# Forty projection tiles in blocks of seven half-depth products in place of eight

## The reference, cut to what matters

```python
h = rms_norm(x, norm_g[layer])
proj = h @ w_in[layer]              # 2048 x 1024 @ 1024 x 8704
u_ssm, z_ssm, q, k, v, z_attn, q_mem, z_mem, gate_logits = split(proj)
y = s5_ssm(u_ssm, ...); y = gelu(y); y = y * sigmoid(y @ w_glu + b_glu)
o_ssm = y * silu(z_ssm)
o_attn = dilated_window_attention(q, k, v) * silu(z_attn)
o_mem = softmax(q_mem @ k_mem.T) @ v_mem * silu(z_mem)
gates = sigmoid(gate_logits + b_gate)
merged = gates[0] * (o_ssm @ w_br_ssm) + gates[1] * (o_attn @ w_br_attn) + gates[2] * (o_mem @ w_br_mem)
x = x + merged @ w_out
return rms_norm(x, final_norm_g)
```

## Time and profile before

| | before |
|---|---|
| median of 3 runs | 2456.7 us (2455.96 to 2456.8) |
| span of the profiled execution | 2455.0 us |
| PE busy, granted clock | 99% of the span, 1.00 in all slices |
| DVE, ACT, POOL busy | 57%, 24%, 8% |
| ACT empties tiles 28 to 43 (64 units, SiLU) | first starts at 686.9, last at 1114.8 us |
| ACT empties tiles 44 to 67 (96 units, gates) | first starts at 1122.3, last at 1817.2 us |

### The profile page before, as it was taken

How to read it: one execution, slowest core, us unless ns; L and a number is a source line. 1 busy time by engine, 2 the same in 40 slices (tenths; PEclk the granted TensorE clock), 3 DMA queues, 4 the chain that set the end, 5 groups by cost and what they waited for, 6 DMA issues and landing times.

```text
span 2455.0 us, 31834 instructions
## 1 busy us (share of the span) xinstructions
PE 2438.3 (99%) x12622; PEld 1981.9 (81%) x12622; DVE 1397.7 (57%) x2636; ACT 588.0 (24%) x1275; POOL 190.4 (8%) x328
## 2 busy tenths in 40 slices
PE   9999999999999999999999999999999999999998
PEld 8888888888877777787777788888888888888887
DVE  7356776767734444413544443444345778787785
ACT  5222222222211111113333343333251111110201
POOL 0000000000011111110000000011100000000000
PEclk9999999999999999999999999999999999999999
DMA  8232433343454444442332343477654865857571
GB/s 327 99 93 76 106 114 117 107 120 95 115 151 137 149 160 142 151 156 73 105 134 95 121 147 122 161 228 243 205 206 164 285 182 168 248 177 242 159 233 59
DMA packets 171033, 378.67 MB, mean 154 GB/s; under 512 B 27008, under 2 KB 72164, under 8 KB 163717
## 3 DMA queue, kind: packets, MB, share of 16 engines
q1 hardware_dynamic: 134980, 235.03, 31.0%
q0 software_dynamic: 34864, 139.51, 16.9%
q10 hardware_dynamic: 1040, 2.10, 0.2%
HBM read 245.10 MB, written 131.43 MB: 153 GB/s over the span
## 4 chain that ended last, share of the span: by engine, by line
PE 97%; DVE 1%; ACT 1%; issue 0%; DMA 0%; DVEq 0%; SPq 0%; ACTq 0%
PE bank L137 29%; PE bank L139 29%; PE bank L138 28%; PE bank L2285 2%; PE bank L2328 1%; PE bank L2306 1%; PE bank L2194 1%; PE bank L2197 1%; PE bank L2264 1%; PE bank L2180 1%; PE bank L2242 1%; PE bank L2316 1%; ACT tsc L1188 1%; PE bank L2145 0%; PE bank L2247 0%
## 5 line engine op out<-in xcount | busy, mean ns | idle before, releaser
L137 PE MATMUL bank<-h_hi,w_hi 128*128 128x512 f32 (+1 forms) x2720 | 1083.7, 398 | 1.4 <-DVE h_lo L1434 1.4
L139 PE MATMUL bank<-h_hi,w_lo 128*128 128x512 f32 (+1 forms) x2720 | 1057.4, 389 | 0.0
L138 PE MATMUL bank<-h_lo,w_hi 128*128 128x512 f32 (+1 forms) x2720 | 1056.3, 388 | 0.0
L137 PEld LDWEIGHTS bank<-h_hi,w_hi 128*128 128x128 f32 x2720 | 510.8, 188 | 117.2 <-issue 13.6
L139 PEld LDWEIGHTS bank<-h_hi,w_lo 128*128 128x128 f32 x2720 | 510.7, 188 | 108.1
L138 PEld LDWEIGHTS bank<-h_lo,w_hi 128*128 128x128 f32 x2720 | 511.3, 188 | 103.0 <-issue 1.7
L129 DVE CAST w_hi<-w_raw 128x1024 fp32r<-128x1024 f32 (+1 forms) x121 | 83.3, 688 | 310.1 <-PE bank L139 294.3
L137 PE MATMUL bank<-h_hi 128*128 128x512 f32 (+1 forms) x464 | 172.5, 372 | 2.7 <-issue 1.5
L139 PE MATMUL bank<-h_hi,h_lo 128*128 128x512 f32 (+1 forms) x464 | 170.4, 367 | 0.0
L138 PE MATMUL bank<-h_lo,h_hi 128*128 128x512 f32 (+1 forms) x464 | 170.3, 367 | 0.0
L956 POOL DMA_DIRECT2D proj_d<-ev x160 | 88.9, 556 | 931.5 <-ACT ev L1148 560.1
(11 more groups left out here) (267 smaller groups left out, 2166.6 us busy)
## 6 DMA issues: line engine op xcount, KB each, us to landing
proj_d<-ev POOLq DMA_DIRECT2D x160, 256.0 KB, 2.9
w_raw<-w_in SPq DMA_DIRECT2D x68, 512.0 KB, 4.9
gt<-proj_d POOLq DMA_DIRECT2D x32, 768.0 KB, 7.6
proj_d<-ev POOLq DMA_DIRECT2D x22, 1024.0 KB, 4.9
w_raw<-w_br SPq DMA_DIRECT2D x32, 512.0 KB, 4.2
wx_raw<-w_br SPq DMA_DIRECT2D x32, 512.0 KB, 4.5
o_d<-ev POOLq DMA_DIRECT2D x12, 1024.0 KB, 6.9
ev<-o_d SPq DMA_DIRECT2D x12, 768.0 KB, 4.4
```

Of the source, the lines that this page charges most:

```text
L137: nc.tensor.matmul(out, ah, bh, start=(start and n == 0), stop=False)
L138: nc.tensor.matmul(out, ah, bl, start=False, stop=False)
L139: last = nc.tensor.matmul(out, al, bh, start=False, stop=(stop and n == len(pairs) - 1))
```

## The change

**Blocks.** The 40 tiles are taken in 20 pairs, and the four chunks as two pairs, (3, 2) and (1, 0). Two tiles by two chunks is a block: 40 blocks. A block as a 2 x 2 by 2 x 2 product of half-depth pieces (4 depth steps each) needs eight half-depth products; the change computes seven, of sums and differences of the pieces, and adds up the results. A product is 12 matmuls of 512 columns. Blocks 0 to 7 are the SiLU pairs with chunks (3, 2), blocks 8 to 27 all pairs with chunks (1, 0), blocks 28 to 39 the gate pairs with chunks (3, 2).

**The seven operands made of h** are computed once by POOL, in eight parts of nine operations of 128 x 512 between tiles 6 and 20 (`make_operands`), stored to `hx_d` (14 MB) and loaded back into `h_lo`'s room when the original chunks are used up (`load_operand`), 1 MB each: five at the entry (two are made in place), seven after block 7, seven after block 27. ACT and DVE split each again in two parts of 128 x 1024 (`operand_hi`, `operand_lo`).

**The seven factors made of the weights** are made for each block: SP loads both tiles in one DMA of 1 MB (`load_factors`), POOL makes five sums of 128 x 512 (`sum_factor`), ACT copies seven high parts (`factor_hi`), DVE subtracts seven low parts (`factor_lo`), each into the room of the same product's factor of the block before, once that product is done.

**The results.** Products 3 to 5 are added in PSUM onto those of 0 to 2. ACT copies four raw results (`keep_raw`) and applies four final functions (`finish_part`), DVE makes three sums (`bank_sum`), POOL three more (`outer_sum`) and issues four stores. `raw_out` is counted on `evac_done`, `sum_out` on `scaled`, `wl_done` on `rstd_done`, `ws_done` on `consts`, `mul_done` on `mm_done`, `fn_done` on `kv_out`, `pool_sum` on `v_turned`.

**Side slots.** The eight beats of a tile are now eight slots of a block, each at the end of a product: after product 0, 1, 2, two after 3, and one after 4, 5 and 6.

```diff
+        def slots_in(g):
+            return [j for j in range(8 * NBK) if 4 * g < triples_before(j) <= 4 * (g + 1)]
...
+                def load_factors(b):
+                    n = block_at(b)[0]
+                    if b:
+                        sp.wait_ge(*count(ws_done, NSUM * b))
+                        sp.wait_ge(*count(wl_done, NPR * (b - 1) + 6))
...
+                    sp.dma_start(w_raw[:, :, :, :], w_in[TILES[n][1]:TILES[n][1] + 2].rearrange(
+                        "s p k c -> p s k c")).then_inc(wr_loaded[0], 16)
...
+                for b in range(NBK):
+                    for i in range(NPR):
+                        g = NPR * b + i
+                        if i == 1:
+                            if b + 1 < NBK:
+                                load_factors(b + 1)
...
+                        done = (b, i - 1) if i else (b - 1, NPR - 1)
+                        if done[0] in SWAPS:
+                            sp.wait_ge(*count(mul_done, g))
+                            load_operand(stage_of(done[0]) + 1, done[1])
+                        for j in slots_in(g):
+                            side_slot(j)
```

On POOL, ACT and DVE each product is followed by fixed work (`after_product`), then by the slots. POOL's:

```diff
+                def outer_sum(b, part):
+                    s1 = ring[:, BUF_C22, :]
+                    if part == 0:
+                        pool.wait_ge(*count(raw_out, 4 * b + 2))
+                        pool.wait_ge(*count(sum_out, 3 * b + 1))
+                        nc.gpsimd.tensor_tensor(s1, s1, ring[:, BUF_C11, :], ALU.add).then_inc(pool_sum[0], 1)
...
+                def after_product(b, i):
+                    if i == 0 and b:
+                        store_part(b - 1, 3)
+                    if i == 2:
+                        outer_sum(b, 0)
+                    if i == 4:
+                        outer_sum(b, 1)
+                    if i == 5:
+                        outer_sum(b, 2)
+                        store_part(b, 0)
+                    if i in (1, 2, 3, 4, 6) and b + 1 < NBK:
+                        sum_factor(b + 1, {1: 0, 2: 2, 3: 3, 4: 4, 6: 6}[i])
+                    if i == 6:
+                        store_part(b, 1)
+                        store_part(b, 2)
```

ACT's:

```diff
+                def after_product(b, i):
+                    if i == 1:
+                        keep_raw(b, 1)
+                        keep_raw(b, 0)
+                    if i == 4:
+                        keep_raw(b, 4)
+                        finish_part(b, 0)
+                    if i == 5:
+                        keep_raw(b, 5)
+                    if i == 6:
+                        for part in (1, 2, 3):
+                            finish_part(b, part)
+                    if i >= 2 and b + 1 < NBK:
+                        for w in {2: (0, 1), 3: (2, 3), 4: (4,), 5: (5,), 6: (6,)}[i]:
+                            factor_hi(b + 1, w)
```

DVE's:

```diff
+                def bank_sum(b, part):
+                    s1, s4 = ring[:, BUF_C22, :], ring[:, BUF_C11, :]
...
+                    elif part == 1:
+                        dve.wait_ge(*count(mul_done, NPR * b + 4))
+                        dve.wait_ge(*count(sum_out, 3 * b + 1))
+                        dve.wait_ge(*count(pool_sum, 3 * b + 1))
...
+                def after_product(b, i):
+                    if i in (2, 3, 6):
+                        bank_sum(b, (i - 2) % 3 if i < 6 else 2)
+                    if i == 0 and 0 < b < NBK:
+                        factor_lo(b, 6)
+                    if i >= 3 and b + 1 < NBK:
+                        for w in {3: (0, 1), 4: (2, 3), 5: (4,), 6: (5,)}[i]:
+                            factor_lo(b + 1, w)
```

What each product waits for on PE:

```diff
+                def product_ready(b, i):
+                    if b == 0 and i < 3:
+                        pe.wait_ge(evac_done, (unit(N_Z - 1, 2), unit(N_Z - 1, 3), unit(N_Z - 1, 1))[i] + 1)
+                    elif i < 2:
+                        pe.wait_ge(*count(raw_out, 4 * (b - 1) + 3 + i))
+                    elif i == 2:
+                        pe.wait_ge(*count(sum_out, 3 * (b - 1) + 3))
+                    elif i < 5:
+                        pe.wait_ge(*count(raw_out, 4 * b + 2))
+                    else:
+                        pe.wait_ge(*count(sum_out, 3 * b + i - 4))
+                    pe.wait_ge(*count(wl_done, NPR * b + i + 1))
```

More of the change, by code:

```diff
@@ L887, in _ @@
                                 load_quarter(0, quarter)
-                        for half in range(2):
-                            beat = 8 * (n - N_GATE) + 2 * c + half
-                            attention_beat(beat)
-                            memory_beat(beat)
-                sp.wait_ge(mm_done, unit(NT - 1, 1) + 1)
+                    beat = j - 8 * (N_GATE - N_Z)
+                    attention_beat(beat)
+                    memory_beat(beat)
+                for n in range(2):
+                    load_tile(n + 2)
@@ L1126, in keep_chunk @@
                     src = bank_of(n, c)[:, :]
[L1127 to L1141 removed]
+                    if c == 0 and n >= 2:
+                        act.wait_ge(stored[s], 16 * (n // 2))
@@ new lines, in finish_part @@
+                def finish_part(b, part):
+                    n = block_at(b)[0]
+                    i, row = ((BUF_C11, 0), (BUF_C21, 1), (BUF_C12, 0), (BUF_C22, 1))[part]
+                    if part == 0:
+                        act.wait_ge(*count(sum_out, 3 * b + 2))
+                    elif part == 3:
+                        act.wait_ge(*count(sum_out, 3 * b + 3))
+                    else:
+                        act.wait_ge(*count(raw_out, 4 * b + part + 2))
+                        act.wait_ge(*count(pool_sum, 3 * b + part + 1))
+                    y = ring[:, i, :]
+                    kind, tile, _ = TILES[n + row]
@@ L1142, in keep_chunk @@
                     if kind == "silu":
-                        ins = nc.scalar.activation(dst, src, ACT.Silu)
-                    elif kind == "gate":
+                        ins = nc.scalar.activation(y, y, ACT.Silu)
+                    else:
                         t = tile - T_G
```

469 lines of the change are left out of this document (361 added, 108 removed).

## The result

| | before | changed |
|---|---|---|
| median (four runs each, side by side) | 2456.3 us (2455.3 to 2456.8) | 2655.3 us (2647.5 to 2658.2) |
| ratio, 95% interval | | 1.0807 (1.0791 to 1.0823) |
| profiled span | 2455.0 us | 2654.3 us |

The account below looks back on a forecast made before the run. The prediction took PE, busy 99% of the span, as the bound: 2455.0 - 108.8 + 18 + 14 + 6 + 10 + 4 + 8 + 1 + 1 = 2408.2, with 1.7 added 2410 us; range 2364 to 2450.

Parts of the forecast that it names:

- The saving: All blocks, on PE: seven half products instead of eight, 480 matmuls of 0.227 us fewer, 108.8 us saved.
- The scan stage: Twelve scan blocks: PE waits some 1.5 us each behind the factors' load and POOL's sums; +18 us.
- POOL and DVE hold each other up: Scan, attention, memory: POOL's sums and DVE's two-SBUF-input operations exclude each other; 36 us more, 2446 in all; chance 0.2.
- Tiles 6 to 20: Operand making: POOL's 72 operations run beside DVE's tables, with some 7 us to spare; +1 us (0 to 12).
- POOL's chain sets the block: Scan blocks, then all 40: POOL's slow operations set the time; some 2470 us at 3 us each; chance 0.08.
- Entry: Before block 0: ACT's copies queue behind two sines, low parts come 1 to 3 us late; +4 us (0 to 8).
- Attention: Attention turns: six lose cover for ACT's exponentials, +14 us; late work or raw copies elsewhere, +6 us (0 to 15).
- Swaps: After blocks 7 and 27: DVE short of time for new operands' low parts, 7 MB arriving late; +10 us (0 to 20).
- Memory stage: Memory stage: 1 MB of factors lands late and waiting POOL holds back stores; +8 us (0 to 20).
- The end: First GLU tiles: h is split a little later, covered by PE's first two chunks; +1 us.
- The clock: Whole kernel: granted clock stays at 1.00 through PE waits of 1 to 3 us; otherwise the mechanism is wrong; no term.
- my 62 us of terms: Whole kernel: all forecast waits together, scan stage, attention, swaps, entry, memory stage, tiles 6 to 20 and end; 62 us.

Follow-up runs that it names:

- e9: Changed kernel with result buffers changing roles, POOL's block sums cut to a few columns and the 72 operand sums left out: 2437.9 us, ratio 0.992.
- e4: Changed kernel with result buffers changing roles and POOL's sums after block 0 cut to a few columns: 2467.1 us, ratio 1.005.
- e3: Changed kernel with POOL's sums after block 0 cut to a few columns, buffers unchanged: 2487.5 us, ratio 1.012.
- e1: Changed kernel with three of four result buffers changing roles from block to block, sums full: 2593.8 us, ratio 1.056.
- e2: Changed kernel without POOL's 72 sums for the operands of h, stores of the same size kept: 2616.0 us, ratio 1.066.
- e5: Changed kernel with role-changing buffers and small block sums, plus ten POOL memsets ahead of each small sum: 2503.6 us, ratio 1.020.
- e11: Kernel before, PE pausing at each of the last 39 tiles' starts for two in-place ScalarE copies: 2559.6 us, ratio 1.0415.
- e12: Kernel before, PE pausing at each of the last 39 tiles' starts for five in-place ScalarE copies: 2671.2 us, ratio 1.0875.

## Why the prediction was wrong, point by point

Two steps failed most. The sum took POOL's new arithmetic as time beside DVE that costs nothing but its own latency in one chain of twelve blocks; measured, it is worth 127 us in the blocks (80 to 90 of them DVE's standstill) and 30 at the tables. And it priced waits at their length, at full clock; measured, they cost 1.4 to 1.5 times that.

**The saving, 108.8: right.** 480 matmuls are gone and the distance at full clock is 0.23 still. e9 reaches 2437.9, since 90 us of the saving are lost elsewhere.

**The scan stage, +18: wrong.** The ten blocks of it named under e4 alone lose 66.3 us. The load that I counted came about as counted: in the block shown it is issued at 848.1, 11.5 us after the block's first matmul (10.1 forecast), and POOL has it at 856.0, 19.3 us (18.7). POOL's operation has 1.29 to 1.51 us (1.23 taken). But I asked only what PE's products wait for, and not what the copy before them waits for. The row of ACT's order with `block_stored0` stood in my own text; the last store of the block before had three products' time and their slots' (8.2 us and the side work; 12.3 in the block shown, from 836.62) for ScalarE's function, its issue and its landing. In that block the three stores are issued only from 844.76 on, behind POOL's sums, and stores landed in 5.7 us median (2.9 before). The page's list of DMA issues (count, KB, median us to landing):

```profile
proj_d<-ev POOLq DMA_DIRECT2D x160, 256.0 KB, 5.7
```

Its price is 20 to 62 us (e4 against e3, e1 against the changed kernel), in all stages; in the ten scan blocks it is about 1 us once POOL's sums are small (e3).

**Rival "POOL and DVE hold each other up", 36 us: the mechanism was right, the size was not.** Shown by e2, e5 and the rows of 5.38 us. I took half an operation for each meeting, and only seven steps a block in one chain. Measured are 80 to 90 us in the blocks and 30 at the tables. Two steps failed: one operation of DVE stood over two of POOL's sums (3.85 us), not for half of one, and operations of DVE outside the chain are hit too, down to the smallest. The Trainium skill's rule (SBUF — State Buffer, "Who interferes with whom": the second to start blocks until the first is done) agrees with the row at 843.67, which ends 0.55 us after POOL's sum. The second operation in the row at 914.41 goes further: it stands for two more of POOL's sums, and no run here shows why POOL came first both times.

**Tiles 6 to 20, +1 (0 to 12): wrong by 29.** I said that POOL's 72 operations run beside DVE's tables and gave them no meeting at all, while I priced meetings in the blocks. e2 puts 30 us on it.

**Rival "POOL's chain sets the block".** It was named as the slower case, from 2.8 us an operation on. POOL's operation has half of that; the chain's latency is 36 us (e5), 48 by the estimate above, and the result is slower mostly for another reason. The rival's own sum was off as well: 1.5 + 5 (x - 1.23) us in each of 12 blocks, with the other 44 us of terms, reach 108.8 at x = 2.0 and not 2.8, and at x = 3 give some 2516 and not 2470.

**Entry, +4 (0 to 8): at the upper end of its bounds**, 7.1 before block 0 and 1.6 in it (e9, where the tables are on time).

**Attention, +14 and +6: near in sum only without POOL's sums**, 19 in e9 up to block 26 and 45 in the changed kernel, and by luck: PE waits for the exponentials 12 times, 23.6 us in all, not six times (with POOL's sums 14 times and 38.2 us, above), and my terms had no clock in them. The list of waits of e9:

```profile
PE bank L2633 <- ACT tsc L1448: 23.6, 12, 6.1
```

**Swaps, +10: too small**, 14.5 for the first and up to 23 for the second with the end of attention (not separated). **Memory stage, +8 (0 to 20): too large without POOL's sums**, 1.5 in e9, and too small with them, 27 in the changed kernel (blocks 30 to 35). **The end, +1: wrong**, 23 in e9 and 44 in the changed kernel: the last factors' load stands behind GLU's loads. The first chunks' cover that I named comes after that wait.

**The clock.** I wrote that I would be wrong if it did not stay at 1.00 through waits of 1 to 3 us. It did not; no term carried it. It makes waiting cost 1.4 to 1.5 times its length in the mean (the changed kernel; e11, e12), so even my 62 us of terms were sized without it.

## What to carry to other kernels

When a change puts work behind a wait, list for each instruction that PE waits for what it waits for itself, down to the store that frees its buffer, and ask what makes that store late. Arithmetic on POOL beside a DVE that works in SBUF is not free time: count it as DVE's time, and test it with a run that nearly leaves it out. And price waits of 2 to 4 us of a full PE at one and a half times their length, as measured here.

## What the runs showed of the hardware that I had not expected

- POOL's 128 x 512 float32 sum: 1.29 us at the least mean (L1121), 1.39 for the factors, 1.51 for three of the operands' nine (the largest mean); a memset of 128 x 56 has 0.15.
- DVE's sums, casts and scalings with all inputs in SBUF stood while POOL's sums ran: 0.157 us became 1.140 (128 x 4), 0.68 became 1.57 (low part of `w_raw`), a pair of 1.29 became 5.38; one operation of 128 x 512 stood over two of POOL's sums, 3.85 us. With one input in PSUM: 0.68, unchanged. A reduction of 128 x 512 that reads SBUF: 0.686, unchanged, though it began 17 times inside a sum. Low parts beside POOL's memsets: unchanged.
- Stores of 256 KB landed in 5.7 us (median of 160) where three of four are issued together; 2.9 before, where they were issued one by one. In the order of issue the medians are 2.7, 4.9, 7.2 and 7.4 us; without POOL's sums all 160 have 4.8 (e4).
- After waits of PE of 4 us and more, the pauses mostly 24 to 38 us apart, the granted clock fell to 1.2 GHz for a stretch each time (29 of 29), after waits of 2.1 us in nine of 20, after waits of 0.9 to 1.2 us in none of nine: 39 pauses with 3.7 us of waiting cost 5.5 us each, 39 with 1.8 us (70.3 in all) cost 2.7.
